# First block of a two-block layer stack: matmuls on x times the norm's weight, with each token's root multiplied onto what leaves PSUM, and x loaded amid the first weights

## The reference, cut to what matters

```python
def rmsnorm(x, g):
    xf = x.astype(jnp.float32)
    y = xf * lax.rsqrt(jnp.mean(xf * xf, axis=-1, keepdims=True) + EPS)
    return (y * g.astype(jnp.float32)).astype(x.dtype)

def swiglu_ffn(x, w_gate, w_up, w_down):
    return (jax.nn.silu(x @ w_gate) * (x @ w_up)) @ w_down

x = x + 0.5 * swiglu_ffn(rmsnorm(x, ffn1_norm[l]), ffn1_w_gate[l], ...)
x = x + hybrid_mixer(rmsnorm(x, mix_norm[l]), w_in[l], ...)
x = x + 0.5 * swiglu_ffn(rmsnorm(x, ffn2_norm[l]), ffn2_w_gate[l], ...)
return rmsnorm(x, final_norm)
```

## Time and profile before

| | us |
|---|---|
| median of 3 runs | 1805.23 |
| lowest, highest | 1804.44, 1809.19 |
| the profiled execution's own time | 1803.77 |
| its span, first to last instruction | 1802.0 |
| PE busy | 1701.6 (94%) |
| ACT, POOL, DVE busy | 683.1, 672.4, 636.1 |

### The profile page before, as it was taken

How to read it: one execution, slowest core, us unless ns; L and a number is a source line. 1 busy time by engine, 2 the same in 40 slices (tenths; PEclk the granted TensorE clock), 3 DMA queues, 4 the chain that set the end, 5 groups by cost and what they waited for, 6 DMA issues and landing times.

```text
span 1802.0 us, 22561 instructions
## 1 busy us (share of the span) xinstructions
PE 1701.6 (94%) x8076; PEld 1393.8 (77%) x8076; DVE 636.1 (35%) x1046; ACT 683.1 (38%) x975; POOL 672.4 (37%) x295
## 2 busy tenths in 40 slices
PE   6999999999999999999999988889898999999997
PEld 5888888878886677888888877677677778877876
DVE  2222320124126723222220126473636341463223
ACT  4344432235236643344342234334242423233431
POOL 4444444443331034444444433232222223444443
PEclk9999999999999998999999988899999999999998
DMA  4233223233220012332232221212121112322321
GB/s 144 93 98 100 93 94 104 94 115 118 72 92 25 1 36 70 95 103 93 93 100 98 93 82 59 71 60 69 47 69 58 58 53 80 124 93 84 103 93 70
DMA packets 41521, 148.70 MB, mean 83 GB/s; under 512 B 4608, under 2 KB 4608, under 8 KB 41216
## 3 DMA queue, kind: packets, MB, share of 16 engines
q1 hardware_dynamic: 39968, 141.58, 23.8%
q10 hardware_dynamic: 1504, 6.45, 1.1%
HBM read 144.86 MB, written 2.10 MB: 82 GB/s over the span
## 4 chain that ended last, share of the span: by engine, by line
PE 65%; issue 24%; POOL 5%; DVE 3%; ACT 1%; DMA 0%; POOLq 0%; DVEq 0%; SPq 0%; ACTq 0%
PE ps L473 15%; PE ps L475 15%; PE ps L474 15%; POOL w_lo L412 5%; PE ps L543 4%; PE ps L545 4%; PE ps L544 4%; PE ps L481 2%; PE ps L717 1%; PE ps L707 1%; PE ps L695 1%; PE ps L488 1%; DVE scr L1449 1%; DMA x<-in_x 0%; ACT h_hi L1060 0%
## 5 line engine op out<-in xcount | busy, mean ns | idle before, releaser
L412 POOL TENSOR_TENSOR w_lo<-w_raw,w_hi 128x1024 fp32r<-128x1024 f32 x262 | 634.5, 2422 | 964.7 <-ACT w_hi L1040 964.7
L1040 ACT ACTIVATE w_hi<-w_raw 128x1024 fp32r<-128x1024 f32 x260 | 275.6, 1060 | 933.3 <-PE ps L475 740.6
L473 PE MATMUL ps<-h_hi,w_hi 128*128 128x512 f32 x1504 | 600.5, 399 | 22.7 <-POOL w_lo L412 9.7
L474 PE MATMUL ps<-h_lo,w_hi 128*128 128x512 f32 x1504 | 591.7, 393 | 0.0
L475 PE MATMUL ps<-h_hi,w_lo 128*128 128x512 f32 x1504 | 591.4, 393 | 0.0
L473 PEld LDWEIGHTS ps<-h_hi,w_hi 128*128 128x128 f32 x1504 | 286.7, 191 | 91.1 <-issue 17.6
L475 PEld LDWEIGHTS ps<-h_hi,w_lo 128*128 128x128 f32 x1504 | 286.0, 190 | 61.0
L474 PEld LDWEIGHTS ps<-h_lo,w_hi 128*128 128x128 f32 x1504 | 286.8, 191 | 58.5
L1459 DVE TENSOR_TENSOR hid<-silu,ps 128x512 f32<-128x512 f32 x44 | 30.3, 688 | 305.6 <-PE ps L475 305.6
L543 PE MATMUL ps<-hid_hi,w_hi 128*128 (+1 forms) x352 | 137.2, 390 | 0.0
L545 PE MATMUL ps<-hid_hi,w_lo 128*128 (+1 forms) x352 | 137.0, 389 | 0.0
(11 more groups left out here) (282 smaller groups left out, 1656.5 us busy)
## 6 DMA issues: line engine op xcount, KB each, us to landing
w_raw<-in_units SPq DMA_DIRECT2D x262, 512.0 KB, 3.3
x<-in_x SPq DMA_DIRECT2D x4, 512.0 KB, 8.1
w<-in_w ACTq DMA_DIRECT2D x1, 2048.0 KB, 8.0
out<-x SPq DMA_DIRECT2D x8, 256.0 KB, 2.0
scr<-proj ACTq DMA_DIRECT2D x8, 128.0 KB, 4.5
inv_count<-in_inv_count ACTq DMA_DIRECT2D x1, 1024.0 KB, 5.0
const<-in_const ACTq DMA_DIRECT2D x1, 899.0 KB, 7.5
q_sc<-in_row_const ACTq DMA_DIRECT2D x1, 512.0 KB, 4.2
```

Source lines behind the costliest of these rows:

```text
L412: nc.gpsimd.tensor_tensor(w_lo[:, slot, :], w_raw[:, slot, :], w_hi[:, slot, :].bitcast(F32), ALU.subtract).then_inc(w_lo_done, 1)
L473: nc.tensor.matmul(ps[:, bank, :], whi, hi[:, k, :], start=(n == 0), stop=False)
L474: nc.tensor.matmul(ps[:, bank, :], whi, lo[:, k, :], start=False, stop=False)
L1040: nc.scalar.activation(w_hi[:, slot, :], w_raw[:, slot, :], ACT.Copy).then_inc(w_hi_done, 1)
```

## The change

Norms 0, 1 and 2 no longer make a normed input. ACT makes `h_hi` from x times the norm's weight (`raw_head`), DVE `h_lo` (`raw_tail`), chunk by chunk as x is ready. Squares of chunks 1 to 7 are all added up on DVE (`add_square`). PE starts the layer's first unit at once; behind it stand the four one-column matmuls (`column_sums`), and behind the second unit the spreading (`row_of_roots`). ACT copies the spread root into `r_row` in SBUF. DVE multiplies `r_row` onto each result: gate and up tile in the feed-forward layers (Silu now goes from `silu` back to PSUM), and all 23 tiles of the projections, which ACT took before. The first four projection tiles use banks 2 to 5. For x and the weights at the start, SP issues x, unit 0, x, x, unit 1, x, then the constants from `dist` on; ACT loads the rest of them. `duplicate` stands one unit later. Norms 3, 4 and 5 are as before, and so is the second block.

```diff
@@ SP, start
-            for c in range(0, DC, 2):
-                sp.dma_start(x[:, c:c + 2, :], ...).then_inc(x_in[c // 2], 16)
-            for u in range(2):
-                sp.dma_start(w_raw[:, u, :], dram["units"][u]).then_inc(raw_full[u], 16)
+            stream(0)
+            weights(0)
+            stream(2)
+            stream(4)
+            weights(1)
+            stream(6)
+            sp.dma_start(const[:, FIRST_CONST:], dram["const"][:, FIRST_CONST:]).then_inc(rest_in, 16)
@@ PE
+            def column_sums(n):
+                pe.wait_ge(sqsum_done, n + 1)
+                add_squares(0, 0, scr[:, 0, :], True, True).then_inc(ssq_done, 1)
+
+            def row_of_roots(n):
+                pe.wait_ge(rstd_done, n + 1)
+                spread_columns(1, r_col).then_inc(spread_done, 1)
...
+                            tile_unit(unit(u0 + 2 * f + m, 4, i), 4 + 2 * f + m, h_hi, h_lo,
+                                      raw(norm_of) if first and f == m == 0 else None)
+                            if first and f == 0:
+                                (row_of_roots if m else column_sums)(norm_of)
...
-                squares_of_half(norm_of + 1, True)
+                if sums_inside:
+                    squares_of_half(norm_of + 1, True)
...
-                    pe.wait_ge(proj_done, u + 1)
+                    if u >= 4:
+                        pe.wait_ge(proj_done, 2 + (u - 3 if u < 6 else u - 1))
+                    tile_unit(unit(U_PROJ + u), project_bank(u), h_hi, h_lo, raw(1) if u == 0 else None)
+                    if u == 0:
+                        column_sums(1)
+                    elif u == 1:
+                        row_of_roots(1)
@@ ACT
+            def raw_head(n, c, gain):
+                if n:
+                    act.wait_ge(x_done, DC * n + c + 1)
+                else:
+                    act.wait_ge(x_in[c // 2], 16)
+                nc.scalar.activation(h_hi[:, c, :], x[:, c, :], ACT.Copy, scale=p_(gain, c, c + 1)).then_inc(raw_hi_done, 1)
...
+                        if first and f == 0:
+                            root(norm_of)
+                            root_row(norm_of)
+                            head(unit(u0 + 2 * f + 3, 4, i))
+                        act.wait_ge(scaled_done, FT * n + 2 * i + f + 1)
+                        nc.scalar.activation(ps[:, 4 + 2 * f, :], silu[:, f, :], ACT.Silu).then_inc(silu_done, 1)
...
+                if gain is not None:
+                    streams(4, 8)
+                    head(unit(ud + 2 * kps + 1))
+                    squares(norm_of + 1, 4, 8)
...
+            def to_stream(u0, n, gain):
+                for c in range(DC - 1):
+                    head(unit(u0 + c + 2))
+                    if c < HPG:
+                        raw_head(n, c, gain)
+                    squares(n, c, c + 1)
+                act.wait_ge(unit_done, u0 + DC)
+                for c in range(HPG, DC):
+                    raw_head(n, c, gain)
+                head(unit(u0 + DC + 1))
+                squares(n, DC - 1, DC)
...
+            for c in range(DC):
+                if c in (2, 6):
+                    first_head(c // 4)
+                raw_head(0, c, "g_ffn1")
+            squares(0, 0, DC)
@@ DVE
+            def raw_tail(n, c, gain):
+                dve.wait_ge(raw_hi_done, DC * n + c + 1)
+                nc.vector.scalar_tensor_tensor(h_lo[:, c, :], x[:, c, :], p_(gain, c, c + 1), h_hi[:, c, :].bitcast(F32),
+                                               ALU.mult, ALU.subtract).then_inc(raw_lo_done, 1)
+
+            def add_square(n, c):
+                dve.wait_ge(sq_done, DC * n + c + 1)
+                ins = nc.vector.tensor_tensor(scr[:, 0, :], scr[:, 0, :], scr[:, c, :], ALU.add)
+                if c < DC - 1:
+                    chain.link(ins)
+                else:
+                    ins.then_inc(sqsum_done, 1)
...
+                        nc.vector.tensor_tensor(silu[:, f, :], ps[:, 4 + 2 * f, :], r_row[:, :], ALU.mult
+                                                ).then_inc(scaled_done, 1)
...
+                        chain.link(nc.vector.tensor_tensor(silu[:, f, :], ps[:, 5 + 2 * f, :], r_row[:, :], ALU.mult))
+                        nc.vector.tensor_tensor(hid[:, f, :], ps[:, 4 + 2 * f, :], silu[:, f, :],
                                                 ALU.mult).then_inc(hid_done, 1)
...
+                    if gain is not None:
+                        raw_tail(next_norm, 4 * half + 3, gain)
+                        for c in range(max(1, 4 * half), 4 * half + 4):
+                            add_square(next_norm, c)
...
+                take(0, 5)
...
+                take(15, 17)
                 for h in range(0, NH, 2):
+                    if h % 4 == 0:
+                        take(17 + h // 2, 19 + h // 2)
                     dve.wait_ge(cmp_pe, 5 + h)
                     nc.vector.tensor_copy(pc_t[:, h, :], ps[0:NCMP, 4 + h % 4, :]).then_inc(pct_done[0], 1)
+                take(21, MTILES)
```

More of the change, by code:

```diff
@@ L1006, in output @@
                 norm(5, "first")
-            pe.wait_ge(small_in, 32)
-            norm(0, "last")
-            ffn(U_FFN1, 0, 0)
-            norm(1, "before")
+            pe.wait_ge(param_in, 16)
+            pe.wait_ge(small_in, 16)
+            ffn(U_FFN1, 0, 0, False)
             project()
@@ L1015, in _ @@
                       lambda k: (o_lo_done, k + 2) if k < HPG else (go_lo, k - HPG + 1))
-            norm(2, "first")
-            ffn(U_FFN2, 1, 2)
+            ffn(U_FFN2, 1, 2, True)
             norm(3, "before")
@@ L1058, in norm, with ffn, pair @@
                 for c in range(DC if parts else 0):
-                    act.wait_ge(hn_done, DC * at + c + 1)
+                    act.wait_ge(hn_done, c + 1)
                     nc.scalar.activation(h_hi[:, c, :], scr[:, c, :], ACT.Copy).then_inc(hn_hi_done, 1)
-            def ffn(u0, n, next_norm):
-                with act.Fori(0, FT // 2) as i:
+            def ffn(u0, n, norm_of, gain):
+                def pair(i, first=False):
                     for f in range(2):
                         head(unit(u0 + 2 * f + 2, 4, i))
-                        act.wait_ge(unit_done, u0 + 4 * i + 2 * f + 1)
-                        act.wait_ge(hid_done, FT * n + 2 * i + f + 1)
-                        nc.scalar.activation(silu[:, f, :], ps[:, 4 + 2 * f, :], ACT.Silu).then_inc(silu_done, 1)
-                        head(unit(u0 + 2 * f + 3, 4, i))
+                        if first and f == 0:
[4 more added lines that the diff above has]
+                        nc.scalar.activation(ps[:, 4 + 2 * f, :], silu[:, f, :], ACT.Silu).then_inc(silu_done, 1)
+                        if not (first and f == 0):
+                            head(unit(u0 + 2 * f + 3, 4, i))
                         act.wait_ge(hid_done, FT * n + 2 * i + f + 3)
@@ L1072, in ffn, with streams @@
                                              hid[:, f, :], ACT.Copy).then_inc(hid_hi_done, 1)
+                pair(0, True)
+                with act.Fori(1, FT // 2) as i:
+                    pair(i)
                 ud = u0 + 2 * FT
                 kps = FT // 2
+                def streams(lo, hi):
+                    if gain is not None:
+                        for c in range(lo, hi):
+                            raw_head(norm_of + 1, c, gain)
                 with act.Fori(0, kps // 2) as i:
@@ L1085, in ffn @@
                 load_root()
-                squares(next_norm, 4, 8)
-                head(unit(ud + 2 * kps + 1))
+                if gain is not None:
[3 more added lines that the diff above has]
+                else:
+                    squares(norm_of + 1, 4, 8)
+                    head(unit(ud + 2 * kps + 1))
             def project():
@@ L1465, in ffn @@
                                                 ALU.subtract).then_inc(hid_lo_done, 1)
+                    chain.leave(FT // 2)
                 for half in range(2):
@@ L1473, in ffn, with take @@
                                                        ALU.mult, ALU.add).then_inc(x_done, 1)
-                    if half == 0:
-                        norm_sum(next_norm)
+                        if gain is not None and d % 4:
+                            raw_tail(next_norm, d - 1, gain)
+                    if gain is not None:
+                        raw_tail(next_norm, 4 * half + 3, gain)
+                        for c in range(max(1, 4 * half), 4 * half + 4):
+                            add_square(next_norm, c)
+                    elif half == 0:
+                        norm_sum(next_norm)
+            def take(first, end):
+                for u in range(first, end):
+                    dve.wait_ge(unit_done, U_PROJ + u + 1)
+                    if MT_GQ <= u < MT_Q + HPG:
+                        dst = queries[:, u - MT_Q, :] if u >= MT_Q else tile_(u)
+                        ins = nc.vector.scalar_tensor_tensor(dst, ps[:, project_bank(u), :], DH ** -0.5, r_row[:, :],
```

(25 more changed lines are left out.)

160 lines of the change are left out of this document (88 added, 72 removed).

## The result

| | before | after |
|---|---|---|
| median of 13 runs each, us (lowest to highest) | 1805.23 (1799.83 to 1811.36) | 1796.25 (1794.02 to 1801.26) |
| ratio, 95% interval | | 0.9948 (0.9935 to 0.9961) |
| profiled execution, its span | 1803.77, 1802.0 | 1797.42, 1795.6 |
| mean granted clock of PE | 0.972 | 0.969 |

The change saves 9.0 us, 0.5%; forecast were 10.2 us and 1795.0. Timed twice more, beside other kernels, the changed kernel stood at 0.9945 (0.9924 to 0.9966) and 0.9949 (0.9930 to 0.9969) of the kernel before.

A forecast was written before the change was run, and what follows sets the result against it. PE is busy 94% of the span, so time comes back only where PE waits or runs slowly. 9.2 + 2.1 + 1.5 - 1.5 - 1.1 = 10.2 us gained gives 1795.0; the 8-in-10 range is 1785 to 1802.

The forecast's parts named there:

- Norm 2: Third unit behind norm 2 starts 14.0 us after the dense work ends, in place of 23.2: gain 9.2 us.
- D: The moment the dense work ahead of a norm ends, from which the prediction timed every step there.
- the case given a bound of 6.5: At norm 2, PE's clock falls in between: spreading 0.9 us longer, a cold unit 1.8 longer, gain only 6.5.
- Norm 1: POOL tail delays the fourth addition and the half clock follows; 1.2 us there plus 0.9 from dropped squares: gain 2.1.
- rival 1: POOL's tails don't get between DVE's additions, so DVE is through first: gain 17.5 us, 1787.7; chance 18%.
- The start: At the kernel's start, with loads reordered, the third unit begins at 35.5 us against 37.05: gain 1.5.
- the prediction's list of signs: What the profile after should show, such as a PE wait of 6 us behind the start's first unit.
- Feed-forward loops: In 44 tiles, two more DVE multiplications each, 61 us of DVE, but PE needs the banks two units on: cost 0.
- Projections: DVE takes 23 tiles from ACT: 1.5 us lost behind unit 18 and 1.1 at the attention's start, 2.6 together.
- rival 3: DVE becomes the bound of the projections and PE waits for its tiles: 7.0 us slower, 1812.2; chance 6%.
- the attention's start: Two bias tiles stand behind tile 22 and the first Exp comes later: loss 0.5 to 1.8 us, taken at 1.1.
- The sum: Whole kernel: 9.2 + 2.1 + 1.5 - 1.5 - 1.1 = 10.2 us gained, giving 1795.0.

The follow-up runs named there:

- the last experiment: The changed kernel run again unedited, beside other kernels: medians 1799.15 and 1799.98 us.
- the first kernel edited: Changed kernel with ACT making the row of roots before the next weight head, norm 2's last square before its head: 1788.43 us; over runs 1793.43 against 1799.98.
- The second experiment: Changed kernel with x split for norm 1 ahead of the weight head in the first FFN's middle: 1796.01 us; over runs 1800.24 against 1799.98.

## Why the prediction was right, point by point

- **Norm 2, 9.2 forecast.** D was 694.33; the POOL tail held the one addition as forecast, and PE waited 1.18 (forecast 1.06). The clock then fell in the second unit (0.74), the case given a bound of 6.5: 7.6 gained. In the second trace of the changed kernel (its first run of the last experiment) it didn't fall: D is the first row's 702.60, sums at D+6.8 (forecast 6.5), third unit at D+14.05 (forecast 14.0), a gain of 9.2.

```profile
702.60 0.39 PE L486 MATMUL ps<-h_hi,w_hi 128*128 128x512 f32 x1
...
709.38 1.05 PE L494 MATMUL ps<-const,scr 128*128 128x1 f32 x8 [1.18 <-DVE scr L1518]
716.65 0.48 PE L486 MATMUL ps<-h_hi,w_hi 128*128 128x512 f32 x1
```

- **Norm 1, 2.1 forecast.** Three additions, the tail, the fourth: as forecast from the earlier trace rows. The last one starts at 391.9 and lasts 2.71 us, beside the tail from 391.61 (view of the line from 387 to 395: count, ns as min/median/max, first and last start):

```profile
L1518 DVE TENSOR_TENSOR scr<-scr x4: 691/1586/2711, 387.9 to 391.9; 128x512 f32<-128x512 f32 x4
```

Sums at D+9.9 (10.2), second unit 6.94 (7.2), third unit at D+18.75 (20.3): 2.7 gained, where this part of the 2.1 was 1.2. The clock came back sooner than assumed (sums 1.26, not 1.7), and the first kernel edited shows the alternative, rival 1, as a matter of order in ACT's queue.
- **The start, 1.5 forecast.** First dense matmul at 11.50 (11.5), first unit's end 19.6 (18.6), additions' end 24.4 (25.4), third unit 34.4 (35.5): 2.7. PE's wait behind the first unit was 4.92; the prediction's list of signs says 6, but its own times, 18.6 and 25.4, make 6.8. The gain comes in spite of the new load order, not by it; the prediction costed the two together and never asked what each does alone. Of `raw_tail` and the additions it found that they decide, but not that they start later if x is. Its 1.3 us for a load of 512 KB is not in the earlier trace rows; it fits the 380 to 439 GB/s that the trace before has from 3 to 13 us.
- **The missed step.** The prediction said nothing of the middle of the first FFN. There norm 1's splits now stand behind `head`, which waits for a unit's end; the split's tail on DVE meets POOL's (2.38 instead of 0.74), the x updates, the next splits and so the next head come late, and PE waits 1.83; by the landmarks 2.1 us of the lead are lost there. The second experiment moved the splits, and the wait was gone. By its own rule (what is queued behind a waiting instruction) it was to be seen: before, only squares stood there.
- **Feed-forward loops, 0 forecast.** DVE's busy time rose from 636.1 to 700.0, the two new multiplications take 44 by 0.69 each, and from 35 to 318 us PE is busy for all of the time, with as many instructions (1250) as before. The lead over the kernel before is 2.3 us at the POOL tails of every unit from 52 to 324 us.
- **Projections, 2.6 lost forecast.** The wait behind unit 18 was 1.46 (1.5) and no other over 1 us came, so rival 3 is out. At the attention's start 1.49 stands in place of 0.51, 1.0 (forecast 1.1). What was not forecast is the clock: a unit behind the compressed scores ran at 1.00 where before it had 0.76, 1.6 gained, and the attention lost 1.5 at 542 to 553 and another 1.5 at 603 to 609.
- **The sum.** 10.2 against 9.0 by the medians and 6.4 by the profiled pair. In the pair, what was not in the sum: the missed wait (-1.8), the clock at norm 2 (-1.6) and in the attention (-3.0), the clock behind the compressed scores (+1.6), the better start and norm 1 (+2.7); together -2.1. The other 1.7 lie in small steps of 0.1 to 0.7, by which the lead shrinks in the units right behind the start, the missed wait and norm 1, and between norm 2 and the end; their cause stays open. The mechanisms of the waits were right but for one; that the median came so near is partly chance, as half of the misses are clock, and the clock behind the compressed scores, a gain here, was a loss in both later traces of the same kernel (3.4 us of half clock by the estimate, against 1.7 before).

## What to carry to other kernels

Where an engine's queue has a long step that holds another engine's port (here a head whose tail on POOL blocks DVE), put whatever the critical chain needs ahead of it; three such moves and the load order brought more than the change itself. Start the inputs of the engine that decides first, not those of the engine whose utilisation one watches. Ask of each moved step what it stands behind at every call, also at the one in the middle of the layer before, and when single traces differ by several microseconds compare waits and landmarks before comparing times. A gain of 2 us was not told from nothing by 6 to 10 runs of each kernel here.

## What the runs showed of the hardware

- **A waiting POOL instruction gets its turn between two DVE instructions of a chain.** Four additions took 6.68 us with a tail that began among them, and 4.66 with none; seven took 7.22 and 5.04. The Trainium skill, "SBUF — State Buffer", section "SBUF: two separate sides", says that whoever starts first has the ports for its whole instruction; the traces agree.
- **PE's clock falls differently in executions of one kernel.** Five of the six stretches above changed their granted clock by 0.23 to 0.40 between two executions of one program, and the estimated cost of the half clock went from 38.8 to 45.2 us. The Trainium skill, "TensorE: Matmul & The Clock Gate", Part 1, says that the gate's watching runs freely and doesn't start with the kernel; this agrees with the traces, and no run here tests it. What work in front makes a fall likely, beyond that it came behind waits and small matmuls, stays open.
